# Modulation units moved from the first FFN steps into the first MLP, chunk-by-chunk block starts, and down products two steps behind

## The chip, the cores and the metric

The kernel runs on one core of a Trainium2 chip. The metric is the time of one launch on the device in microseconds, as the median of several runs. The profile shows one further execution of the same program.

## The reference, cut to what matters

`x` has 256 tokens of 1,024 features, all in float32. A first block stack runs over it, then a second one with modulation from a condition vector:

```python
def swiglu(h, w13, w2):
    gate, up = jnp.split(h @ w13, 2, axis=-1)
    return (jax.nn.silu(gate) * up) @ w2
...
x = x + 0.5 * swiglu(rms_norm(x, ffn1_norm[l]), ffn1_w13[l], ffn1_w2[l])   # four FFNs in all, hidden 2816
...
mod = (sc @ w_mod[l] + b_mod[l])[:, None, :]            # sc = silu(c), w_mod[l] is 1024 x 6144, l = 0, 1
sh1, sc1, g1, sh2, sc2, g2 = jnp.split(mod, N_MOD, axis=-1)
...
mod_c = scc @ w_mod[l] + b_mod[l]                       # the context's own modulation, l = 0, first two parts
...
h = h + g1 * y
h = h + g2 * sq_relu_mlp(modulate(rms_norm_2(h, norm2_g[l]), sh2, sc2), w_mlp1[l], w_mlp2[l])  # hidden 4096
```

Between the FFNs stand a recurrent block and a stick-breaking attention; in the second stack, a Fourier and neighbourhood-attention mixer (`l = 0`) and a pooling mixer (`l = 1`), each followed by an MLP.

## The kernel before, in words

**Products.** Features lie on the 128 partitions, in 8 chunks, and tokens on the free axis. Every float32 product is made of three reduced-precision matmuls: high part of the weight by high and by low part of the operand, then low part of the weight by high part (`product`, lines 1471 to 1480). The parts come by splitting: ScalarE writes the rounded high part (`w_hi`, L421), VectorE subtracts it for the low part (`w_lo`, L828).

**The stream.** All weights stand in one stream of 576 units of 128 x 1024 values, in the order of use. SyncE loads them in pairs of 1 MB into a ring of 8 units (`raw`, L348); `w_hi` and `w_lo` are rings of 8 too. A unit's `w_hi` is written only once TensorE has begun the next product unit after the one that had the slot (`unit_used`, `split_hi`). `unit_ready` makes TensorE wait for `w_lo`. Both engines work through the units in order: `pump_to(n)` splits all units up to n, and is written out by hand between the other work of the engine.

**An FFN.** It has 22 steps (`FFS`). Step j has two up units (gate and up columns, 24 matmuls each, `up`), then one down unit (24 matmuls, `down`). Of the up result VectorE makes `t2` with the norm's `rstd` (L965), ScalarE the silu (L479), VectorE the product (L968), ScalarE its high part (L481) and VectorE the low part `hid_lo` (L970): together the hidden tile of step j (`hidden`). The order on TensorE is up j, down j-1: the down product is one step behind. The up results go to PSUM banks 4 and 5 in turn, hidden tiles to two slots, the down sums to banks 0 to 3. `FF_ORDER` lays the units out.

**Block start.** `update_and_operand` (VectorE) and `gain_operand` (ScalarE) add the last block's result to `x` and make the operand of the next one chunk by chunk (`u_hi` L451, `u_lo` L928; L915 in `ffn0` and `ffn2`, L941 in the MLPs), while GpSimd adds up ScalarE's squares (L377, L379). `up(0)` takes its first unit chunk by chunk as the operands arrive, then `norm_sum` sums the squares over the features (one matmul, L1469, bank 7), then come the second unit and `up(1)`. VectorE and ScalarE make `rstd` of the sum (`rms`: L893, the root L443, then L884 to L887), for which `pump_to` has gone up to unit 3 of the FFN. `q`, the first projection of the attention, uses `by_chunk`: of each operand chunk the products of four units are made before the next chunk is taken.

**Modulation.** The two 1024 x 6144 matrices make 96 units of the stream, four to a group of 512 columns, 24 groups. TensorE does not see them: VectorE multiplies the unit's two halves by the condition and adds them to an accumulator, one multiply-add of 128 x 512 to each half (L836 the first, L837 the others, `modulate`); for the context's modulation each half is taken once more (4 groups of `l = 0`). At the end of a group TensorE sums the accumulator over the partitions (`sum_modulation`, four small matmuls, L1547), and VectorE adds the bias (`read_modulation`, L1003). Each FFN has 24 of these units, from step 2 on, in steps 2 to 9 two and one in turn, then one a step (`MODS_AT`); the sums come after the down products of steps 4, 6, 8, 12, 16 and 20. The context's groups are the third and the fourth of `ffn0` and `ffn1`.

**An MLP.** 16 steps (`MLS`) of two up and two down units, matmuls of 258 columns: the two extra ones carry the shift. Up j, down j-1; the up results lie in banks 4 to 7, two each in turn. `sqrelu` starts like an FFN, with `norm_sum` behind the first unit. VectorE reads the shift column (L1036), scales (L1037), ScalarE does the relu (L521), VectorE the square (L1040), then high part (L524) and low part (L1042). There are no modulation units in it.

## Time and profile before

| | us |
|---|---|
| median of 3 runs (1698.51 to 1702.51) | 1699.18 |
| the profiled execution | 1701.26 |
| its span, first to last instruction | 1699.4 |
| TensorE busy (95%) | 1609.3 |
| VectorE busy (71%) | 1200.9 |
| ScalarE busy (46%) | 784.7 |
| GpSimd busy (3%) | 47.0 |

The stretch from the first to the last instruction is the span; the time of a run has some 2 us around it. An engine's busy time is the time in which an instruction of it runs. Matmuls overlap, so the mean duration of one is longer than the distance from one to the next. The granted clock is 1.00 where TensorE runs at 2.4 GHz and 0.50 where it runs at 1.2 GHz; its mean over the span is 0.972.

### The profile page before, as it was taken

To read this page: it belongs to the slowest core of one execution; us is meant where nothing else is said; L and a number is where in the kernel's file an instruction comes from. 1 tells how busy PE (TensorE), PEld (TensorE's weight loads), DVE (VectorE), ACT (ScalarE), POOL (GpSimd) and SP (SyncE) were. 2 spreads that over 40 slices of the span, in tenths; PEclk is the share of its full clock that TensorE was granted. 3 is DMA by queue.
4 is the path that set the end of the run, shared out by engine and by line. 5 is a ranking of instruction groups with operands and counts; after the bars stand their busy time and mean duration, and the time that the engine had idled before them with its cause. 6 is when DMAs were issued, how large, how long until landed. Compare 5 with 4: busy or idle time off the path is not lost.

```text
span 1699.4 us, 30213 instructions
## 1 busy us (share of the span) xinstructions
PE 1609.3 (95%) x12406; PEld 1532.0 (90%) x12406; DVE 1200.9 (71%) x1660; ACT 784.7 (46%) x1121; POOL 47.0 (3%) x46
## 2 busy tenths in 40 slices
PE   6999996899999899999899999998799999889999
PEld 6999996899999799999679999995368999889999
DVE  6887788888878577787767777744757565576654
ACT  5434457543445343445654344422445444454442
POOL 1000010100001100001010000000001000010000
PEclk9999998899999899999999999998899999999999
DMA  6766643466666356565225656531224445334550
GB/s 262 265 245 242 227 169 128 149 250 246 243 231 225 143 198 263 224 233 197 98 100 198 261 223 238 210 124 44 68 87 176 183 173 191 106 122 176 179 191 25
DMA packets 43433, 310.82 MB, mean 183 GB/s; under 512 B 4816, under 2 KB 5072, under 8 KB 6096
## 3 DMA queue, kind: packets, MB, share of 16 engines
q1 hardware_dynamic: 41904, 303.33, 48.0%
q0 software_dynamic: 864, 5.21, 0.9%
q8 instruction: 61, 1.00, 0.2%
q10 hardware_dynamic: 576, 1.05, 0.2%
q14 instruction: 28, 0.23, 0.0%
HBM read 308.52 MB, written 1.05 MB: 182 GB/s over the span
## 4 chain that ended last, share of the span: by engine, by line
PE 67%; DVE 11%; ACT 2%; issue 1%; POOL 0%; POOLq 0%; DVEq 0%; ACTq 0%
PE psum L1474 20%; PE psum L1479 20%; PE psum L1480 20%; DVE w_lo L828 3%; DVE buf L837 1%; ACT w_hi L421 1%; PE psum L1926 1%; PE psum L1649 1%; PE psum L1637 1%; PE psum L1547 1%; DVE u_lo L928 1%; DVE x L907 1%; PE psum L1748 0%; DVE tiny L1380 0%; PE psum L1462 0%
## 5 line engine op out<-in xcount | busy, mean ns | idle before, releaser
L1474 PE MATMUL psum<-u_hi,w_hi 128*128 128x256 f32 (+2 forms) x2608 | 762.4, 292 | 39.1 <-DVE u_lo L915 14.2
L1479 PE MATMUL psum<-u_lo,w_hi 128*128 128x256 f32 (+2 forms) x2608 | 749.8, 287 | 0.0
L1480 PE MATMUL psum<-u_hi,w_lo 128*128 128x256 f32 (+2 forms) x2608 | 749.5, 287 | 0.0
L828 DVE TENSOR_TENSOR w_lo<-raw,w_hi 128x1024 fp32r<-128x1024 f32 x480 | 565.4, 1223 | 163.1 <-ACT w_hi L421 162.9
L1474 PEld LDWEIGHTS psum<-u_hi,w_hi 128*128 128x128 f32 x2608 | 508.1, 195 | 51.0 <-issue 17.3
L421 ACT ACTIVATE w_hi<-raw 128x1024 fp32r<-128x1024 f32 x480 | 478.2, 1046 | 119.6 <-PE psum L1474 112.7
L1479 PEld LDWEIGHTS psum<-u_lo,w_hi 128*128 128x128 f32 x2608 | 508.3, 195 | 2.0
L1480 PEld LDWEIGHTS psum<-u_hi,w_lo 128*128 128x128 f32 x2608 | 507.7, 195 | 1.3
L1474 PE MATMUL psum<-hid_hi,w_hi 128*128 128x256 f32 x1220 | 346.7, 284 | 7.0 <-DVE hid_lo L1357 3.7
L1479 PE MATMUL psum<-hid_lo,w_hi 128*128 128x256 f32 x1220 | 345.6, 283 | 0.0
L1480 PE MATMUL psum<-hid_hi,w_lo 128*128 128x256 f32 x1220 | 345.6, 283 | 0.0
L1474 PEld LDWEIGHTS psum<-hid_hi,w_hi 128*128 128x128 f32 x1220 | 234.4, 192 | 9.8 <-DVE hid_lo L1357 5.5
L1479 PEld LDWEIGHTS psum<-hid_lo,w_hi 128*128 128x128 f32 x1220 | 234.4, 192 | 0.0
L1480 PEld LDWEIGHTS psum<-hid_hi,w_lo 128*128 128x128 f32 x1220 | 234.4, 192 | 0.0
L479 ACT ACTIVATE buf<-buf 128x256 f32<-128x256 f32 x88 | 36.8, 418 | 367.5 <-DVE buf L965 367.5
L837 DVE SCALAR_TENSOR_TENSOR buf<-raw,tiny,buf 128x512 f32<-128x512 f32 x196 | 143.4, 749 | 4.1
L965 DVE TENSOR_TENSOR buf<-psum,rstd 128x512 f32<-128x512 f32 x88 | 60.5, 687 | 30.6 <-PE psum L1480 30.4
L970 DVE TENSOR_TENSOR hid_lo<-buf,hid_hi 128x256 fp32r<-128x256 f32 x88 | 37.5, 426 | 42.7 <-ACT hid_hi L481 42.7
L968 DVE TENSOR_TENSOR buf<-buf 128x256 f32<-128x256 f32 x88 | 37.4, 426 | 42.6 <-ACT buf L479 42.6
L377 POOL TENSOR_TENSOR buf<-buf 128x512 f32<-128x512 f32 x27 | 35.6, 1317 | 1143.4 <-ACT buf L439 1141.0
L521 ACT ACTIVATE buf<-buf,tiny 128x256 f32<-128x256 f32 x64 | 29.1, 502 | 72.8 <-DVE buf L1037 72.8
L481 ACT ACTIVATE hid_hi<-buf 128x256 fp32r<-128x256 f32 x88 | 36.8, 419 | 43.3 <-DVE buf L968 43.3
(224 smaller groups left out, 982.2 us busy)
## 6 DMA issues: line engine op xcount, KB each, us to landing
raw<-stream SPq DMA_DIRECT2D x288, 1024.0 KB, 4.8
buf<-tab POOLq DMA_DIRECT2D x2, 768.0 KB, 4.6
x<-x_in SPq DMA_DIRECT2D x1, 1024.0 KB, 7.0
buf<-ctx_in POOLq DMA_DIRECT2D x1, 1024.0 KB, 5.1
buf<-poolmat POOLq DMA_DIRECT2D x1, 1024.0 KB, 5.0
out<-x ACTq DMA_DIRECT2D x4, 256.0 KB, 2.4
cst<-consts POOLq DMA_DIRECT2D x1, 864.0 KB, 9.1
buf<-late POOLq DMA_DIRECT2D x1, 640.0 KB, 4.5
```

The source lines that it names most:

```text
L377: gp.tensor_tensor(a, a, buf[4][:, half(b)], ALU.add).then_inc(S.pool_sum, 1)
L421: sc.activation(w_hi[:, u], raw[:, u], ACT.Copy).then_inc(S.hi_ready, 1)
L479: sc.activation(sil, t2[:, 0:T], ACT.Silu).then_inc(S.gated, 1)
L481: sc.activation(hid_hi[:, j % 2, 0:T], h32[:, 0:T], ACT.Copy).then_inc(S.hid_hi_ready, 1)
L828: ve.tensor_tensor(w_lo[:, u], raw[:, u], w_hi[:, u].bitcast(F32), ALU.subtract).then_inc(S.lo_ready, 1)
L837: return ve.scalar_tensor_tensor(acc, w, c, acc, ALU.mult, ALU.add)
L965: ve.tensor_tensor(t2.rearrange("p (k t) -> p k t", k=2), bank2(4 + par), over2(rstd[:, :]), ALU.mult).then_inc(S.up_scaled, 1)
L968: ve.tensor_tensor(h32[:, 0:T], sil, t2[:, T:2 * T], ALU.mult).then_inc(S.hid_f32, 1)
L970: ve.tensor_tensor(hid_lo[:, par, 0:T], h32[:, 0:T], hid_hif[:, par, 0:T], ALU.subtract)\
L1474: ins = te.matmul(dst, w_hi[:, w], hi, start=first, stop=False, skip_group_check=True)
L1479: te.matmul(dst, w_hi[:, w], lo, start=False, stop=False, skip_group_check=True)
L1480: return te.matmul(dst, w_lo[:, w], hi, start=False, stop=last, skip_group_check=True)
```

## The change

The groups of modulation units are listed by hand (`GROUPS`) and given to the blocks by `HOME`: 4, 4, 5 and 5 groups to the FFNs, 6 to `mlp0`. In the FFNs they begin at step 6 (in `ffn2` and `ffn3` with two a step in steps 6 to 9, else one), in `mlp0` two a step in steps 3 to 14. The context's groups are the first two of `ffn0` and `ffn1`. In `mlp0` the sums go to column 300 of a bank of the up product just read, and `up_pair` waits for the read of it.

In the FFNs down j-2 comes after up j (`LAG`), the hidden tiles have four slots, and the third up pair has bank 7. `ffn1` to `ffn3` take their first four units chunk by chunk, `ffn0` its first two, the MLPs their first three. `norm_sum` comes after the block, in `ffn0` after `up(1)`, and in these blocks into bank 0. ScalarE and VectorE split the units up to number 7 of an FFN before the root. The scale `G2` is made after `ffn3` instead of after `ffn1`, `H2` after `mlp0`.

```diff
-FFU = 4 * FFS + 2
-MODG = 6
-MODS_AT = [0, 0] + [2, 1] * 4 + [1] * (FFS - 10)
...
+LAG = 2
+GROUPS = [(0, 0), (0, 1), (0, 4), (0, 5), (0, 2), (0, 3), (0, 6), (0, 7), (0, 8), (0, 9), (0, 10), (0, 11)]
+GROUPS += [(1, _n) for _n in range(12)]
+HOME = {"ffn0": range(0, 4), "ffn1": range(4, 8), "ffn2": range(8, 13), "ffn3": range(13, 18), "mlp0": range(18, 24),
+        "mlp1": range(24, 24)}
+CTX_GROUPS = [[0, 1], [4, 5]]
+MODS_AT = {"ffn0": [0] * 6 + [1] * 16, "ffn1": [0] * 6 + [1] * 16, "ffn2": [0] * 6 + [2] * 4 + [1] * 12,
+           "ffn3": [0] * 6 + [2] * 4 + [1] * 12, "mlp0": [0] * 3 + [2] * 12 + [0], "mlp1": [0] * MLS}
+SUM_AT = {"ffn0": [8, 12, 16, 20], "ffn1": [8, 12, 16, 20], "ffn2": [6, 8, 12, 16, 20], "ffn3": [6, 8, 12, 16, 20],
+          "mlp0": [3, 5, 7, 9, 11, 13], "mlp1": []}
+ORDER = {}
+for _name, _mods in MODS_AT.items():
+    assert sum(_mods) == 4 * len(HOME[_name])
+    _lag, _wide = (LAG, 1) if _name[:3] == "ffn" else (1, 2)
+    ORDER[_name] = []
+    for _j, _m in enumerate(_mods):
+        ORDER[_name] += [("up", _j)] * 2 + [("mod", _j)] * _m + [("down", _j - _lag)] * (_wide * (_j >= _lag))
+    for _j in range(len(_mods) - _lag, len(_mods)):
+        ORDER[_name] += [("down", _j)] * _wide
...
-MOD_COLS = [[4, 5, 0, 1, 6, 7], [8, 9, 2, 3, 10, 11], [0, 1, 2, 3, 4, 5], [6, 7, 8, 9, 10, 11]]
...
+def unit_at(name, kind, j):
+    return AT[name] + ORDER[name].index((kind, j))
...
+def end_of(name):
+    return AT[name] + len(ORDER[name])
...
+MOD_ACC, MOD_FREE = {}, {}
+for _name, _groups in HOME.items():
+    for _i, _g in enumerate(_groups):
+        MOD_ACC[_g] = _i % 2 if _name == "mlp0" else int(_i >= len(_groups) - 3)
+        MOD_FREE[_g] = max([g + 1 for g in range(_g) if MOD_ACC[g] == MOD_ACC[_g]], default=0)
 MOD_BACK = {}
...
@@ -113,7 +131,7 @@
 RD = {n: i for i, n in enumerate("ffn0 rec gate wout ffn1 k v ffn2 wo ffn3 k2 fq2 v2 woe mlp0 pool mlp1".split())}
 NORMS = "start ffn0 wout ffn1 ctx ffn2 wo ffn3 woe mlp0 pool".split()
 NRM = {n: i for i, n in enumerate(NORMS)}
-NORM_BANK = {"ffn3": 0}
+NORM_BANK = {n: 0 for n in ("start", "wout", "ctx", "wo", "ffn3", "woe", "pool")}
...
+UP_BANK = [4, 5, 7] + [4 + _j % 2 for _j in range(3, FFS)]
+MOD_COL = 300
...
         hid_hif = hid_hi_t[:, :].bitcast(F32).rearrange("p (s t) -> p s t", s=2)
+        ff_hi = hid_hi_t[:, :].rearrange("p (s t) -> p s t", s=4)
+        ff_lo = hid_lo_t[:, :].rearrange("p (s t) -> p s t", s=4)
...
-                    sc.activation(hid_hi[:, j % 2, 0:T], h32[:, 0:T], ACT.Copy).then_inc(S.hid_hi_ready, 1)
-                pump_to(c0 + ff_at("down", 0) - 1)
+                    sc.activation(ff_hi[:, j % 4, :], h32[:, 0:T], ACT.Copy).then_inc(S.hid_hi_ready, 1)
                 for j in range(FFS - 2):
                     hidden(j)
-                    pump_to(c0 + ff_at("down", j + 1) - 1)
...
                 for j in range(MLS):
                     hidden(j)
-                    pump_to(min(c0 + 4 * j + 5 + AHEAD, last - 1))
+                    pump_to(min(unit_at(name, "up", j + 1) + 1 + RING, last - 1) if j + 1 < MLS else last - 1)
...
@@ -551,7 +574,7 @@
                 square(0, x_t, b)
                 if b == 1:
                     pump_to(3)
-            pump_to(ff_at("down", 0) - 1)
+            pump_to(7)
...
             pump_to(AT["ffn1"] + AHEAD - 1)
-            gain_operand("ffn2_0", "wout", early=AT["ffn1"] + 4)
+            gain_operand("ffn2_0", "wout", early=AT["ffn1"] + 8)
...
@@ -778,6 +801,7 @@
             norm_only("mlp0")
+            act.wait_ge(S.mod_read, HOME["mlp0"][-1] + 1)
             shift_operand(1)
             v = ck(buf[3])
...
-                    ve.tensor_tensor(hid_lo[:, par, 0:T], h32[:, 0:T], hid_hif[:, par, 0:T], ALU.subtract)\
+                    ve.tensor_tensor(ff_lo[:, j % 4, :], h32[:, 0:T], ff_hif[:, j % 4, :], ALU.subtract)\
                       .then_inc(S.hid_ready, 1)
-                pump_to(c0 + ff_at("down", 0) - 1)
                 for j in range(FFS - 2):
                     hidden(j)
-                    pump_to(c0 + ff_at("down", j + 1) - 1)
-                    if j in MOD_READ:
-                        read_modulation(MODG * int(name[3]) + MOD_READ.index(j))
+                    pump_to(unit_at(name, "down", j) - 1)
+                    if j in SUM_AT[name]:
+                        read_modulation(HOME[name][SUM_AT[name].index(j)])
                     if name == "ffn2" and CTX_FROM <= j <= CTX_FROM + NC:
                         context_operand(j - CTX_FROM)
                 hidden(FFS - 2)
-                read_modulation(MODG * int(name[3]) + MODG - 1)
-                pump_to(c0 + FFU + 3)
+                pump_to(end_of(name) - 1)
+                read_modulation(HOME[name][-1])
+                pump_to(end_of(name) + 3)
                 hidden(FFS - 1)
...
@@ -1043,7 +1061,10 @@
                 for j in range(MLS):
                     hidden(j)
-                    pump_to(min(c0 + 4 * j + 5 + AHEAD, last - 1))
+                    pump_to(min(unit_at(name, "up", j + 1) + 1 + RING, last - 1) if j + 1 < MLS else last - 1)
+                    if j in SUM_AT[name]:
+                        read_modulation(HOME[name][SUM_AT[name].index(j)], 4 + 2 * (j % 2), MOD_COL)
...
+            pump_to(7)
...
-            pump_to(AT["ffn1"] + 3)
+            pump_to(AT["ffn1"] + 7)
...
@@ -1416,6 +1439,8 @@
             sqrelu("mlp0")
+            modulation_done("mlp0")
+            scale_gain("H2", 1, 4, "n2_1")
             update_x("mlp0", lambda k: part(0, 5, k))
...
@@ -1466,7 +1491,12 @@
                 pe.wait_ge(S.ssq_ready, POOL_SUMS[name] + 1)
                 if n == 0:
                     pe.wait_ge(S.consts_in, 16)
-                te.matmul(psum[:, 7, 0:T], ones, buf[4][:, 0:T], start=True, stop=True).then_inc(S.ms_psum, 1)
+                if name == "ctx":
+                    pe.wait_ge(S.v_out, 1)
+                te.matmul(psum[:, NORM_BANK.get(name, 7), 0:T], ones, buf[4][:, 0:T], start=True, stop=True)\
+                  .then_inc(S.ms_psum, 1)
...
-            def by_chunk(c, op, dsts, done):
+            def by_chunk(c, op, dsts, done, w=T, shared=True):
                 unit_ready(c + len(dsts) - 1)
@@ -1498,8 +1526,9 @@
                     operand(op, k)
                     for s in range(len(dsts)):
-                        ins = product(dsts[s], c + s, k * P, u_hi[:, k, 0:T], u_lo[:, k, 0:T],
-                                      k == 0 and s % 2 == 0, k == NC - 1, begins=k == (NC - 1 if s else 0))
+                        ins = product(dsts[s], c + s, k * P, u_hi[:, k, 0:w], u_lo[:, k, 0:w],
+                                      k == 0 and (s % 2 == 0 or not shared), k == NC - 1,
+                                      begins=k == (NC - 1 if s else 0))
                         if k == NC - 1 and s % 2:
                             ins.then_inc(done, 1)
                 begun[0] = c + len(dsts) - 1
...
-            def up(c, i, j, par, h0, op=None, between=lambda: None):
-                if not isinstance(j, int) or j >= 2:
+            def up(c, i, j, bank, h0):
+                if not isinstance(j, int) or j > 2:
                     pe.wait_ge(S.up_scaled, h0 + j - 1)
-                all_k(c, i, bank2(4 + par)[:, 0, :], op)
-                between()
-                all_k(c + 1, i, bank2(4 + par)[:, 1, :]).then_inc(S.up_ready, 1)
+                all_k(c, i, bank2(bank)[:, 0, :])
+                all_k(c + 1, i, bank2(bank)[:, 1, :]).then_inc(S.up_ready, 1)
...
             def swiglu(name, norm):
-                c0, h0, g0 = AT[name], STEPS[name], MODG * int(name[3])
-                def down(j, par, c, i=0, first=False, last=False):
+                c0, h0, groups = AT[name], STEPS[name], HOME[name]
+                def down(j, slot, c, i=0, first=False, last=False):
                     pe.wait_ge(S.hid_ready, h0 + j + 1)
-                    one_k(c, i, hid_hi[:, par, 0:T], hid_lo[:, par, 0:T], 0, first, last)
-                up(c0 + ff_at("up", 0), 0, 0, 0, h0, name, between=lambda: norm_sum(norm))
-                up(c0 + ff_at("up", 1), 0, 1, 1, h0)
-                pe.wait_ge(S.ms_ready, NRM[norm] + 1)
-                down(0, 0, c0 + ff_at("down", 0), first=True)
+                    one_k(c, i, ff_hi[:, slot, :], ff_lo[:, slot, :], 0, first, last)
+                first = [bank2(UP_BANK[j])[:, n, :] for j in range(2) for n in range(2)]
+                if name == "ffn0":
+                    by_chunk(c0, name, first[:2], S.up_ready)
+                    up(c0 + 2, 0, 1, UP_BANK[1], h0)
+                else:
+                    by_chunk(c0, name, first, S.up_ready)
+                norm_sum(norm)
                 for j in range(2, 10):
-                    up(c0 + ff_at("up", j), 0, j, j % 2, h0)
-                    down(j - 1, (j - 1) % 2, c0 + ff_at("down", j - 1))
-                    if j in (4, 6, 8):
-                        sum_modulation(g0 + j // 2 - 2, j // 2 - 2, last_unit(g0 + j // 2 - 2))
+                    up(unit_at(name, "up", j), 0, j, UP_BANK[j], h0)
+                    if j == 2:
+                        pe.wait_ge(S.ms_ready, NRM[norm] + 1)
+                    down(j - 2, (j - 2) % 4, unit_at(name, "down", j - 2), first=j == 2)
+                    if j in SUM_AT[name]:
+                        g = groups[SUM_AT[name].index(j)]
+                        sum_modulation(g, 0, last_unit(g))
                 with pe.Fori(0, (FFS - 10) // 4) as i:
                     for s in range(4):
-                        j, c = 10 + 4 * i + s, c0 + ff_at("up", 10 + s)
-                        up(c, 2 * i, j, s % 2, h0)
-                        down(j - 1, 1 - s % 2, c + 3, 2 * i)
+                        j, c = 10 + 4 * i + s, unit_at(name, "up", 10 + s)
+                        up(c, 2 * i, j, 4 + s % 2, h0)
+                        down(j - 2, s, c + 3, 2 * i)
                         if s == 2:
-                            sum_modulation(g0 + 3 + i, 3, c0 + ff_at("mod", 13), 2 * i)
-                if g0 < 2 * MODG:
-                    sum_context(g0 // MODG)
-                down(FFS - 1, 1, c0 + FFU - 1, last=True)
+                            sum_modulation(groups[-3] + i, 1, unit_at(name, "mod", 13), 2 * i)
+                down(FFS - 2, (FFS - 2) % 4, end_of(name) - 2)
+                if name in ("ffn0", "ffn1"):
+                    sum_context(int(name[3]))
+                down(FFS - 1, (FFS - 1) % 4, end_of(name) - 1, last=True)
...
             def sqrelu(name, norm):
                 c0, h0 = AT[name], STEPS[name]
-                def up_pair(c, i, j, par, op=None, between=lambda: None):
-                    if not isinstance(j, int) or j >= 2:
-                        pe.wait_ge(S.up_scaled, h0 + j - 1)
-                    all_k(c, i, psum[:, 4 + 2 * par, 0:TS], op, TS)
-                    between()
-                    all_k(c + 1, i, psum[:, 5 + 2 * par, 0:TS], w=TS).then_inc(S.up_ready, 1)
-                def down(j, par, c, i=0, first=False, last=False):
+                def up_pair(j):
+                    c, par = unit_at(name, "up", j), j % 2
+                    pe.wait_ge(S.up_scaled, h0 + j - 1)
+                    if j - 2 in SUM_AT[name]:
+                        pe.wait_ge(S.mod_read, HOME[name][SUM_AT[name].index(j - 2)] + 1)
+                    all_k(c, 0, psum[:, 4 + 2 * par, 0:TS], w=TS)
+                    all_k(c + 1, 0, psum[:, 5 + 2 * par, 0:TS], w=TS).then_inc(S.up_ready, 1)
+                def down(j, first=False, last=False):
+                    c, par = unit_at(name, "down", j), j % 2
                     pe.wait_ge(S.hid_ready, h0 + j + 1)
                     for n in range(2):
-                        one_k(c + n, i, hid_hi[:, par, n * T:(n + 1) * T], hid_lo[:, par, n * T:(n + 1) * T], 0,
+                        one_k(c + n, 0, hid_hi[:, par, n * T:(n + 1) * T], hid_lo[:, par, n * T:(n + 1) * T], 0,
                               first and n == 0, last and n == 1)
                 pe.wait_ge(S.shift_lo, 1 if name == "mlp0" else 2)
-                up_pair(c0, 0, 0, 0, name, between=lambda: norm_sum(norm))
+                by_chunk(c0, name, [psum[:, 4 + n, 0:TS] for n in range(3)], S.up_ready, TS, False)
+                norm_sum(norm)
+                all_k(c0 + 3, 0, psum[:, 7, 0:TS], w=TS).then_inc(S.up_ready, 1)
                 pe.wait_ge(S.ms_ready, NRM[norm] + 1)
-                up_pair(c0 + 2, 0, 1, 1)
-                down(0, 0, c0 + 4, first=True)
-                with pe.Fori(0, (MLS - 2) // 2) as i:
-                    for s in range(2):
-                        j, c = 2 + 2 * i + s, c0 + 6 + 4 * s
-                        up_pair(c, i, j, s)
-                        down(j - 1, 1 - s, c + 2, i)
-                down(MLS - 1, 1, c0 + 4 * MLS - 2, last=True)
+                down(0, first=True)
+                for j in range(2, MLS):
+                    up_pair(j)
+                    down(j - 1)
+                    if j in SUM_AT[name]:
+                        g = HOME[name][SUM_AT[name].index(j)]
+                        pe.wait_ge(S.up_scaled, h0 + j + 1)
+                        sum_modulation(g, MOD_ACC[g], last_unit(g), bank=4 + 2 * (j % 2), at=MOD_COL)
+                down(MLS - 1, last=True)
```

## Rows read from the trace of the kernel before

**Rows 1.** The page: TensorE's busy time, and one group of the costliest instructions.

```profile
PE 1609.3 (95%) x12406; PEld 1532.0 (90%) x12406; DVE 1200.9 (71%) x1660; ACT 784.7 (46%) x1121; POOL 47.0 (3%) x46
...
L837 DVE SCALAR_TENSOR_TENSOR buf<-raw,tiny,buf 128x512 f32<-128x512 f32 x196 | 143.4, 749 | 4.1
```

**Rows 2.** Windows; stretch: length, busy PE, PEld, DVE, ACT, POOL; PEclk, DMA share, GB/s.

```profile
10.24:30.88 20.64, 16.68 (x99) 15.47 (x100) 15.48 (x19) 12.43 (x19) 5.49 (x5) 1.00 0.62 256
322.39:340.79 18.40, 15.88 (x99) 14.64 (x99) 14.29 (x20) 8.98 (x16) 4.62 (x4) 0.81 0.21 80
587.12:606.14 19.02, 14.58 (x101) 14.20 (x100) 11.81 (x21) 7.06 (x13) 4.51 (x4) 0.82 0.08 31
886.81:903.91 17.10, 14.99 (x92) 13.96 (x93) 12.94 (x17) 7.63 (x13) 4.62 (x4) 0.80 0.00 0
1282.09:1299.51 17.42, 15.03 (x93) 14.08 (x93) 14.71 (x20) 10.20 (x16) 5.28 (x5) 0.80 0.32 121
1504.50:1521.88 17.38, 14.40 (x101) 13.72 (x100) 14.05 (x22) 8.37 (x14) 4.53 (x3) 0.90 0.35 122
```

**Rows 3.** Windows: whole steps of `ffn0`, `ffn1`, the end of `ffn2`, one MLP step.

```profile
79.00:99.50 20.50, 17.57 (x145) 17.20 (x144) 17.46 (x25) 7.34 (x10) 0.00 (x0) 1.00 0.64 239
100.55:136.53 35.98, 35.98 (x290) 35.98 (x289) 30.02 (x42) 14.72 (x20) 0.00 (x0) 0.95 0.68 235
136.53:171.96 35.43, 35.43 (x298) 35.43 (x297) 26.37 (x35) 15.76 (x22) 0.00 (x0) 1.00 0.67 254
388.69:406.61 17.92, 17.37 (x145) 17.17 (x145) 16.32 (x23) 5.26 (x7) 0.00 (x0) 1.00 0.63 226
407.66:442.59 34.93, 34.65 (x288) 34.45 (x289) 29.44 (x41) 14.32 (x19) 0.00 (x0) 1.00 0.67 236
443.64:478.13 34.49, 34.49 (x290) 34.49 (x289) 26.29 (x35) 15.78 (x22) 0.00 (x0) 1.00 0.71 262
784.34:787.98 3.64, 2.88 (x26) 2.68 (x24) 2.61 (x5) 0.83 (x2) 0.00 (x0) 1.00 1.03 407
1360.00:1371.56 11.56, 11.56 (x98) 11.56 (x98) 6.86 (x11) 5.56 (x7) 0.00 (x0) 1.00 0.50 181
```

**Rows 4.** Timeline of TensorE, starts of `ffn0`, `ffn1`: start, duration, instruction [idle <- releaser].

```profile
19.98 0.58 PE L1474 MATMUL psum<-u_hi,w_hi 128*128 128x256 f32 x1
...
322.39 0.36 PE L1474 MATMUL psum<-u_hi,w_hi 128*128 128x256 f32 x1 [1.47 <-DVE u_lo L928]
...
328.50 0.58 PE L1474 MATMUL psum<-u_hi,w_hi 128*128 128x256 f32 x1 [0.41 <-DVE u_lo L928]
...
330.18 1.05 PE L1469 MATMUL psum<-buf,cst 128*128 128x256 f32 x2
```

**Rows 5.** Timeline of VectorE: first hidden tile of `ffn1`, and a step with context.

```profile
335.34 0.69 DVE L965 TENSOR_TENSOR buf<-psum,rstd 128x512 f32<-128x512 f32 x1
...
337.43 0.42 DVE L970 TENSOR_TENSOR hid_lo<-buf,hid_hi 128x256 fp32r<-128x256 f32 x1 [0.48 <-ACT hid_hi L481]
...
424.19 0.69 DVE L965 TENSOR_TENSOR buf<-psum,rstd 128x512 f32<-128x512 f32 x1
...
433.29 0.68 DVE L965 TENSOR_TENSOR buf<-psum,rstd 128x512 f32<-128x512 f32 x1
```

**Rows 6.** Windows at the lower clock: in `ffn1`'s start and before the pooling mixer.

```profile
326.80:333.60 6.80, 6.11 (x24) 5.48 (x25) 4.36 (x5) 2.81 (x3) 2.06 (x2) 0.50 0.01 4
...
1480.50:1487.30 6.80, 4.33 (x14) 3.56 (x15) 4.18 (x11) 3.58 (x8) 0.00 (x0) 0.50 0.00 0
```

**Rows 7.** Timeline: TensorE before the pooling mixer; `mlp1`'s norm sum and first `hid_lo`.

```profile
1482.97 0.69 PE L1953 MATMUL psum<-cst,buf 128*128 128x128 f32 x2 [5.67 <-ACT buf L787]
...
1511.09 1.14 PE L1469 MATMUL psum<-buf,cst 128*128 128x256 f32 x2 [2.19 <-POOL buf L379]
...
1519.47 0.69 DVE L1042 TENSOR_TENSOR hid_lo<-buf,hid_hi 128x512 fp32r<-128x512 f32 x1 [0.70 <-ACT hid_hi L524]
```

**Rows 8.** Timeline of VectorE in `mlp0`: the last split of a step.

```profile
1381.90 1.23 DVE L828 TENSOR_TENSOR w_lo<-raw,w_hi 128x1024 fp32r<-128x1024 f32 x1 [1.68 <-ACT w_hi L421]
```

125 lines of the change are left out of this document (54 added, 71 removed).

## The prediction

> **What bounds the kernel now.** I read the engines' shares first: TensorE is busy for 95% of the span [rows 1]. The weight splitting and the modulation on VectorE run beside it and cost time only where TensorE waits for them. So the question is where TensorE is idle or slow and how much of that the change removes. The stretches of the six block starts, each from the first up matmul to the first down matmul, come next [rows 2]: to read are the stretch, TensorE's busy time and the granted clock. In `ffn1` 18.40 us pass, 15.88 busy, at a mean clock of 0.81, for 96 up matmuls and one sum. At full rate these are worth some 12: a steady stretch of four FFN steps, 288 matmuls without a modulation sum, takes 34.49 us [rows 3], so 0.1198 us a matmul, 2.87 us a unit of 24, 5.75 us an up pair, 8.62 us a step. With one sum the same stretch takes 35.43 us, so a sum costs 0.94. The MLP's step of 96 matmuls takes 11.56 us, 2.89 a unit [rows 3].
>
> At a start the first unit waits chunk by chunk for operands ([1.47 <- DVE] before the first [rows 4]); then the norm's sum of squares is taken; `rstd` and the first hidden tile must follow before the first down product. From the sum's start at 330.18 [rows 4] to the end of `hid_lo` at 337.85 [rows 5] are 7.67 us. The clock stood at its lower level of 1.2 GHz (granted 0.50) from 326.8 to 333.6 [rows 6]. In `ffn2` and `mlp1` TensorE also waits for GpSimd's sum: `mlp1` shows 2.19 [rows 7], and in `ffn2` busy time falls short of the stretch by 4.44 [rows 2].
>
> **FFN starts (`ffn1`, `ffn2`, `ffn3`).** The change takes four units chunk by chunk: 96 matmuls, 11.50 us, 12 matmuls (1.44 us) to an operand chunk, where one unit alone spent 0.36. Operands for the seventh chunk were there at 328.50, 6.1 us after those of the first [rows 4], 1.0 us a chunk and so faster than 1.44: I expect no gap after the first. Then the norm's sum, then `up(2)` (5.75), then the first down product. The chain from sum to `hid_lo` I take at 7.2: the 7.67 less about half of the sum matmul's 1.05, which ran at the lower clock [rows 4]; ends 7.0 and 7.7. TensorE has sum and `up(2)` to do meanwhile, about 6.3, and idles 0.9. The first down product thus comes 11.50 + 7.2 = 18.7 us after the first up matmul; before it came after 18.40, 19.02 and 17.10 [rows 2]. But one more up pair is done by then, 5.75 us of work. Gain: 5.75 - 0.3 = 5.45, 5.75 + 0.3 = 6.05, 5.75 - 1.6 = 4.15, together 15.7.
>
> What is late next: the second down unit. The chunk block keeps its four ring slots to the end, and ScalarE and VectorE split unit 8 only after the second hidden tile. With H the first `hid_lo`: a hidden tile takes 2.51 (335.34 to 337.85 [rows 5]), unit 8 another 1.05 + 1.23 less 0.4 of overlap, the third tile 2.5, unit 9 again 1.9 to 2.3: ready at about H + 9.4. TensorE wants it after one down and one up pair, H + 8.6. I charge 0.8 three times, 2.4 in all; bounds 0 and 2.87 each. Leaves 13.3. The two extra splits ahead of `rms` fall in the chunk block, where VectorE is free, and cost nothing; if GpSimd's sums held them up, up to 3 us are spare.
>
> **`ffn0` start.** It runs at the lower clock from the beginning; the last operand chunk starts at 19.98 [rows 4]. Only two units go by chunk. Six matmuls at about 0.21 follow it, then `up(1)` 5.75 with some 0.5 for the clock: the sum at 27.7, `hid_lo` at 34.9. Before, the first down product stood at 30.88 with 5.75 us less done: gain 1.7, less the same 0.8, makes 0.9; bounds -1 and 3.
>
> **Modulation out of the first six steps.** A step with one unit that also feeds the context takes VectorE 9.10 us (424.19 to 433.29 [rows 5]) against TensorE's 8.62, or 8.86 with a quarter of a sum. Today the units of `ffn0` and `ffn1` start at step 2, two in every other step, and VectorE comes late at the sum of step 8. Two steps took 20.50 instead of 17.24, and the next four 35.98 instead of 34.49 at a clock of 0.95; in `ffn1` 17.92 instead of 17.24 and 34.93 instead of 34.49 [rows 3]. That is 3.26 + 1.49 + 0.68 + 0.44 = 5.9 us. After the change VectorE enters step 6 with nothing owed and runs eight such steps 0.24 behind each, 1.9 us. A sum needs its last unit 11.3 us after the up pair two steps before (down, up pair, down), and VectorE's hidden tile, three splits and one unit need 9.2: the spare 2.1 just covers it. So all 5.9 are gained; bounds 3 and 5.9.
>
> **Two steps behind at the end.** The last hidden tile today leaves TensorE idle 3.64 - 2.88 = 0.76 in `ffn2` [rows 3], and alike in `ffn3`. With two down units (5.75) in between, against the split that now waits for the last up pair (2.3) and the tile (2.5), that is gone: 1.5.
>
> **MLP starts.** Three units go by chunk, 72 matmuls, 8.7 us, and only then comes the sum. Its chain to `hid_lo`, 1511.09 to 1520.16 [rows 7], is 9.07; half a microsecond less at full clock, 8.6. TensorE has only the sum and one unit, 3.5 us, and idles 5.1. The first down product comes after 17.3 us; before after 17.42 and 17.38 [rows 2]. The idle time is thus moved and not removed. And the clock: around 5.67 us idle before 1482.97 [rows 7] it stood at 0.50 from 1480.5 to 1487.3 [rows 6], 4.3 us of that behind the idle time, half of it lost: 2.2. I charge 2.2 for each MLP, 4.4; bounds 0 and 3.4 each.
>
> The Trainium skill, "TensorE: Matmul & The Clock Gate", section "Why this matters for your kernels", warns of idle gaps between bursts of matmuls as what sets the clock back. By it the new gaps in the MLPs are the harm of this change. The trace agrees in the 5.67 us gap; in `ffn1` it shows a fall with no such gap, and what the page would make of that stands with the second rival.
>
> **Modulation in `mlp0`.** Twelve steps get two units each, four multiply-adds of 0.75 us [rows 1], 3.0 us. VectorE is busy 6.86 of 11.56 now [rows 3]; the rest is waiting, 1.68 of it before one split for a ring slot [rows 8], and about 1.9 for ScalarE. With the units it needs 6.9 + 1.9 + 3.0 and 0.1 for the read, 11.9; TensorE with half a sum needs 12.03. I cost this at nothing: it is hidden by the down product that comes a whole step later (7.7 us spare). The sums only move, 24 in all; so do the DMAs of the stream, six units in 12 us against five in 8.9 us in `ffn2`. `H2`'s scale before the update after `mlp0` lies where VectorE waits for the last product: nothing.
>
> **Sum.** 13.3 + 0.9 + 5.9 + 1.5 - 4.4 = 17.2. The profiled execution took 1701.26 us (span 1699.4), so 1684.1. It was 2.1 above the median of the runs, 1699.18, and by that the median would be 1682.0; for small losses that I can't see in the rows I add 1: **1683**.
>
> **Rivals.**
> - *The MLPs keep their clock.* The 2.19 us gap in `mlp1` [rows 7] went with only half as long a fall as the FFNs (mean clock 0.90 against 0.80 [rows 2]). Against it stands the 5.67 row. 4.4 us less: 1679.
> - *The FFN starts fall to the lower clock all the same.* For it: at 326.8 it fell though the one gap of any length was 1.47, before the first matmul, and that stays [rows 4, 6], so a gap alone may not be the cause. Three times 6.8 us at half rate cost 3.4 each, less what the wait for `hid_lo` hides: 1683 + 10 = 1693. By the page's rule on idle gaps, named above, that fall had no gap to come from, and this rival is what it would make of the time.
> - *VectorE still comes late in the context steps.* If the 2.1 us of spare are not there, the sums of step 8 and 12 stall in both FFNs, or the second down unit waits a whole 2.87: some 7 us, 1690.
> - *Slower: `mlp0` goes at VectorE's pace.* If the 4.70 us in which VectorE idles per step today [rows 3] are fixed waits for ring slots and ScalarE, and do not fill with modulation, its step is 14.56 against 12.03; twelve steps lose 30, less 7.7 of look-ahead, 22: 1705. It decides the sign from a VectorE step of about 14.1 on. Against it: those slot waits end at a fixed point of TensorE's progress, so work put in after them delays the next wait and doesn't add to it.
>
> **Numbers.** The forecast gets 0.58, the clock kept 0.12, the clock lost 0.12, VectorE late 0.12, slower 0.06. A measurement of this kernel tells 0.3% from no change, 5.1 us: faster is below 1694.1. All of the first, second and fourth, and half of the third, lie there: 0.88; no change 0.06, slower 0.06. The range runs from the kept clock with the better bounds, 1677, to the lost clock, 1693.
>
> **What would show it.** Right: in `ffn1` to `ffn3` no idle TensorE between the first up matmul and the norm's sum, the first down product 18.7 us after it, full clock; no stall at a sum in `ffn0`; about 5 us idle in both MLP starts, with granted clock 0.50 behind. Wrong: a fall at the FFN starts; waits of TensorE for `w_lo` at the second down unit beyond 1 us; in `mlp0` steps longer than 12.1 us with TensorE waiting for `hid_lo` or a multiply-add.

## The result, and the profile after

| | before | after |
|---|---|---|
| median of the runs | 1698.85 us (1697.87 to 1702.51, 4 runs) | 1675.49 us (1675.29 to 1677.33, 4 runs) |
| profiled execution | 1701.26, span 1699.4 | 1675.29, span 1673.5 |
| mean granted clock | 0.972 | 0.978 |

The ratio is 0.9855, with a 95% interval of 0.9839 to 0.9871. The change gains 23.4 us by the medians and 25.9 by the spans. The forecast was 16.2 and 1683; 1675.5 lies 1.5 below its range.

The page of the changed kernel, busy time of the engines and the group that answers to the second of [rows 1]:

```profile
PE 1591.8 (95%) x12406; PEld 1520.4 (91%) x12406; DVE 1202.9 (72%) x1660; ACT 783.8 (47%) x1121; POOL 49.1 (3%) x46
...
L861 DVE SCALAR_TENSOR_TENSOR buf<-raw,tiny,buf 128x512 f32<-128x512 f32 x196 | 143.5, 749 | 5.3 <-DVE buf L861 0.5
```

TensorE executes the same 12406 matmuls, and VectorE's work has not changed (1202.9 against 1200.9). So the whole gain is idle time and clock. The clock's part can be estimated from the mean granted clock: 1699.4 x (1 - 0.972) = 47.6 us before, 1673.5 x (1 - 0.978) = 36.8 after. That is some 10.8 of the 25.9. TensorE's idle time by the pages fell by 8.4 (1699.4 - 1609.3 = 90.1 before, 1673.5 - 1591.8 = 81.7 after). The other 6.7 or so must lie in what counts as busy, since matmuls overlap: pauses shorter than the modelled end of one, and the beginning of `ffn0`, for which the clock row is of no use.

The granted clock is on record only from its first change on, and the windows over this beginning say 1.00 in both kernels, while the matmuls themselves come 0.21 us apart up to 22.9 before and up to 13.4 after, and 0.12 apart behind. TensorE's timeline there, two lines of the kernel before, then two of the changed one:

```profile
22.71 0.41 PE L1480 MATMUL psum<-u_hi,w_lo 128*128 128x256 f32 x1
23.08 0.28 PE L1479 MATMUL psum<-u_lo,w_hi 128*128 128x256 f32 x1
...
13.11 0.41 PE L1509 MATMUL psum<-u_lo,w_hi 128*128 128x256 f32 x1
13.62 0.28 PE L1509 MATMUL psum<-u_lo,w_hi 128*128 128x256 f32 x1
```

Windows of the changed kernel over the starts of the four FFNs and of `mlp0`, first up matmul to first down matmul (their edges are up to 0.1 us off those matmuls), in the order of [rows 2] and with its columns:

```profile
10.12:33.80 23.68, 20.26 (x146) 19.32 (x146) 18.29 (x22) 13.46 (x21) 5.54 (x5) 1.00 0.80 315
312.86:331.70 18.84, 17.93 (x146) 17.68 (x146) 14.29 (x20) 9.93 (x17) 4.69 (x4) 1.00 0.37 130
567.63:586.55 18.92, 18.01 (x149) 17.76 (x147) 13.66 (x21) 8.08 (x14) 6.29 (x4) 1.00 0.27 102
858.80:877.60 18.80, 17.89 (x148) 17.63 (x146) 14.21 (x20) 9.84 (x17) 4.70 (x4) 1.00 0.21 76
1247.30:1264.61 17.31, 12.26 (x98) 12.00 (x98) 14.88 (x22) 9.98 (x18) 5.34 (x5) 0.95 0.40 147
```

In `ffn1` 146 matmuls are done in 18.84 us, where 98 were done in 18.40, and the granted clock is 1.00 instead of 0.81. That is the core of the change in one pair of rows.

Windows over the rest of the blocks, first down matmul to the first update of x; first two of the kernel before (`ffn0`, `ffn1`), then the same two, `mlp0` and `mlp1` of after:

```profile
30.88:219.60 188.72, 185.79 (x1538) 185.27 (x1537) 148.56 (x198) 77.42 (x105) 0.00 (x0) 0.99 0.67 249
340.79:525.77 184.98, 184.15 (x1538) 183.75 (x1537) 145.72 (x195) 77.43 (x105) 0.00 (x0) 1.00 0.67 249
```

```profile
33.80:209.96 176.16, 176.09 (x1472) 176.12 (x1472) 134.76 (x177) 76.58 (x104) 0.00 (x0) 1.00 0.62 233
331.70:507.86 176.16, 176.09 (x1472) 176.12 (x1473) 134.76 (x177) 76.58 (x104) 0.00 (x0) 1.00 0.61 233
...
1264.61:1444.42 179.81, 179.16 (x1472) 178.99 (x1473) 135.56 (x175) 81.06 (x105) 0.00 (x0) 0.99 0.65 246
1494.80:1667.74 172.94, 172.87 (x1424) 172.90 (x1425) 98.11 (x116) 78.43 (x101) 0.00 (x0) 0.99 0.41 147
```

Behind the first down product no FFN has an idle TensorE any more: 176.09 busy of 176.16 in `ffn0`, where 2.9 us were missing, and as little is missing in `ffn2` and `ffn3`. `mlp0` now executes six sums more, 5.6 us, and the mean clock behind both MLP starts is 0.99.

TensorE's timeline of the changed kernel in `ffn1` and at the first down products of the MLPs (start, duration, instruction [idle <- releaser]):

```profile
312.86 0.36 PE L1504 MATMUL psum<-u_hi,w_hi 128*128 128x256 f32 x1 [1.47 <-DVE u_lo L951]
...
324.45 0.60 PE L1498 MATMUL psum<-buf,cst 128*128 128x256 f32 x2
...
331.77 0.36 PE L1504 MATMUL psum<-hid_hi,w_hi 128*128 128x256 f32 x1 [0.98 <-issue]
...
1264.69 0.55 PE L1504 MATMUL psum<-hid_hi,w_hi 128*128 128x256 f32 x1 [5.13 <-issue]
...
1494.87 0.55 PE L1504 MATMUL psum<-hid_hi,w_hi 128*128 128x256 f32 x1 [5.16 <-issue]
```

Taking the first down product and the first update of x of each block in both traces as marks, with a unit at 2.87, an up pair at 5.75 and a sum at 0.94 us (forecast, from [rows 3]), the span's gain is made up so:

| part | forecast | measured |
|---|---|---|
| starts of `ffn1`, `ffn2`, `ffn3` | 15.7 - 2.4 = 13.3 | 5.2 + 7.4 + 5.2 = 17.9 |
| start of `ffn0` | 0.9 | 2.8 |
| rest of the four FFNs (modulation, two steps behind) | 5.9 + 1.5 = 7.4 | 4.9 + 1.2 + 0.7 + 0.9 = 7.7 |
| both MLPs | -4.4 | -0.4 - 1.5 = -1.9 |
| all other stages | 0 | -0.6 |
| sum | 17.2 | 25.9 |

(The parts are rounded.) For `ffn1`, for example: its first down product came at 340.79 and 331.77, the update of x before it at 320.50 and 310.97. The stretch between grew by 0.51, with one up pair more in it: 5.75 - 0.51 = 5.24.

### The profile page after: what moved, and what is told of

Same layout as the page of the kernel before. It is cut to its first block, busy times and chain, and to the rows that moved or that the text cites. A ratio compares the mean times of both kernels' runs of the same rounds, so it can differ in the third digit from the quotient of the medians.

```text
span 1673.5 us, 30069 instructions
## 1 busy us (share of the span) xinstructions
PE 1591.8 (95%) x12406; PEld 1520.4 (91%) x12406; DVE 1202.9 (72%) x1660; ACT 783.8 (47%) x1121; POOL 49.1 (3%) x46
## 4 chain that ended last, share of the span: by engine, by line
PE 75%; DVE 5%; issue 1%; ACT 1%; DVEq 0%; ACTq 0%
PE psum L1504 23%; PE psum L1509 22%; PE psum L1510 22%; DVE w_lo L852 1%; PE psum L1576 1%; PE psum L1688 1%; PE psum L1676 1%; PE psum L1965 1%; PE psum L1904 1%; ACT w_hi L444 0%; PE psum L1787 0%; DVE tiny L1403 0%; PE psum L1487 0%; PE psum L1945 0%; PE psum L2004 0%
## 5 line engine op out<-in xcount | busy, mean ns | idle before, releaser
L1504 PE MATMUL psum<-u_hi,w_hi 128*128 128x256 f32 (+2 forms) x2608 | 752.1, 288 | 28.9 <-DVE u_lo L938 12.6
L1504 PEld LDWEIGHTS psum<-u_hi,w_hi 128*128 128x128 f32 x2608 | 501.7, 192 | 36.4 <-issue 17.0
L1509 PEld LDWEIGHTS psum<-u_lo,w_hi 128*128 128x128 f32 x2608 | 501.9, 192 | 1.7
L1510 PEld LDWEIGHTS psum<-u_hi,w_lo 128*128 128x128 f32 x2608 | 501.7, 192 | 1.3
L502 ACT ACTIVATE buf<-buf 128x256 f32<-128x256 f32 x88 | 36.8, 418 | 317.4 <-DVE buf L987 317.4
L504 ACT ACTIVATE hid_hi<-buf 128x256 fp32r<-128x256 f32 x88 | 36.8, 418 | 43.3 <-DVE buf L990 43.3
```

The source lines that it names most:

```text
L502: sc.activation(sil, t2[:, 0:T], ACT.Silu).then_inc(S.gated, 1)
L504: sc.activation(ff_hi[:, j % 4, :], h32[:, 0:T], ACT.Copy).then_inc(S.hid_hi_ready, 1)
L1504: ins = te.matmul(dst, w_hi[:, w], hi, start=first, stop=False, skip_group_check=True)
L1509: te.matmul(dst, w_hi[:, w], lo, start=False, stop=False, skip_group_check=True)
L1510: return te.matmul(dst, w_lo[:, w], hi, start=False, stop=last, skip_group_check=True)
```

## The experiments

All are edits of the changed kernel. Their own medians stand beside the ratio to the kernel before on the same chip, since the kernel before itself had medians of 1699 to 1703 us there; the ratio is the safer of the two. The changed kernel's is 0.9855.

### Each of three parts undone alone

**The old places of the modulation units** (all 96 in the FFNs, from step 2 on):

```
-MODS_AT = {"ffn0": [0] * 6 + [1] * 16, ...
+MODS_AT = {f"ffn{_f}": [0, 0] + [2, 1] * 4 + [1] * 12 for _f in range(4)}
+MODS_AT.update({"mlp0": [0] * MLS, "mlp1": [0] * MLS})
```

> The changed kernel with the modulation units back in steps 2 to 21 of the four FFNs, as before the change (groups, context groups and accumulators too). Theory: the new places are worth the 5.9 us that the rows of ffn0 and ffn1 showed, so 1675.5 + 5.9 = 1681.4, with TensorE waiting at the sum of step 8 in ffn0. Rival A: the down product two steps behind takes up VectorE's lateness by itself, and the places are worth nothing: 1675 to 1677. Rival B: units from step 2 on also collide with the late ring slots behind the chunk block, some 2 us more in each FFN: about 1690.

Measured: 1706.65 us, ratio 1.0037 (1.0024 to 1.0050). Undoing 5.9 us of the forecast cost 31. Timeline of this kernel, the split of the first down unit in `ffn1` (VectorE), then the product that waited for it:

```profile
345.88 3.50 DVE L851 TENSOR_TENSOR w_lo<-raw,w_hi 128x1024 fp32r<-128x1024 f32 x3 [0.52 <-ACT w_hi L444]
```

```profile
347.26 0.55 PE L1502 MATMUL psum<-hid_hi,w_hi 128*128 128x256 f32 x1 [5.19 <-DVE w_lo L851]
```

Part of it comes from how the two edits meet. With down products two steps behind, units at step 2 stand ahead of the first down unit; by the code it became the ninth unit instead of the seventh, so that it needs a slot of the ring again, and its split starts only behind the second hidden tile. TensorE idled 5.19 us in each FFN, and the clock fell at the end of it each time. By the marks of the table above, 17.2 of the 30.4 us of span lie in the four starts and 11.6, besides the sums, in the rest of the FFNs. So this run doesn't price the places alone, and the next one was made for that.

**The old number of units, but none ahead of the first down unit:**

```
+MODS_AT = {f"ffn{_f}": [0, 0, 0] + [2, 2, 2, 2, 1, 2, 1] + [1] * 12 for _f in range(4)}
```

> All 96 modulation units are again in the four FFNs, 12 of each 24 in the steps with index 3 to 9, but none ahead of the first down unit, which stays the seventh unit (with the old places it was the ninth, and its low part came 4.2 us late). Theory by the terms of the forecast (modulation in the early steps costs 5.9, its place at the start is what cost the first experiment the rest): 1675.5 and 5.9, about 1681.5, no idle time of 5 us ahead of the first down products and no fall of the clock there. Second reading (the bodies of the FFNs in the first experiment lost 11.5 us beside their sums): 1687. Rival (modulation in these steps puts VectorE behind whatever its place at the start): 1695 or more.

Measured: 1706.07 us, ratio 1.0024 (1.0013 to 1.0035). The time is the rival's. The starts are as in the changed kernel (0.98 us idle), so the loss is in the rest of the blocks. Windows of this kernel over the same stretch of `ffn0` and `ffn1`, and over 26 us inside `ffn1`:

```profile
33.80:220.78 186.98, 181.49 (x1487) 180.89 (x1488) 146.00 (x196) 76.58 (x104) 0.00 (x0) 0.98 0.64 242
342.48:531.00 188.52, 180.57 (x1486) 179.54 (x1487) 146.14 (x196) 76.58 (x104) 0.00 (x0) 0.99 0.63 240
...
377.00:403.00 26.00, 23.32 (x194) 22.98 (x193) 21.39 (x33) 10.70 (x15) 0.00 (x0) 1.00 0.67 241
```

`ffn1` takes 188.52 us against 176.16, of which 7.95 are an idle TensorE, 1.9 the two sums that came back, and the rest mostly clock. Before the change `ffn1` held as many units and idled 0.83 (184.98 with 1538 matmuls, above). Where TensorE waits is on record too. VectorE's timeline of this kernel in `ffn1`, then a product that waited:

```profile
346.66 0.48 DVE L859 TENSOR_SCALAR buf<-raw,tiny 128x512 f32<-128x512 f32 x1
347.17 2.41 DVE L860 SCALAR_TENSOR_TENSOR buf<-raw,tiny,buf 128x512 f32<-128x512 f32 x3
...
353.90 0.35 PE L1502 MATMUL psum<-hid_hi,w_hi 128*128 128x256 f32 x1 [2.36 <-DVE w_lo L851]
```

The 2.36 stand ahead of the second down unit, and there is such a wait in all four FFNs: two modulation units now lie between it and the first, and their four multiply-adds delay its split. That is the place where the forecast charged its 0.8, and where the changed kernel does not wait. The other waits in `ffn1` (0.23 to 2.19 us) stand ahead of later down products and one sum. So both layouts of the old number collide with the late first down units, each in its own way, and this one packs two units a step into steps 3 to 6 besides, where the kernel before had two and one in turn. Neither shows what the old places would cost without such a collision.

**The same, but with the first six steps free and nothing in `mlp0`:**

```
+MODS_AT = {f"ffn{_f}": [0] * 6 + [3] * 4 + [1] * 12 for _f in range(4)}
```

> The first six steps of each FFN hold no modulation, as in the changed kernel, but nothing goes to mlp0: the steps 6 to 9 take three units each, so that all 24 of an FFN are placed. It tells the two halves of the new placement apart. If leaving the early steps is what counts: near the changed kernel, 1677 to 1681. If VectorE's load in the rest of the FFN decides (9.1 us with one unit and context, 3 us more with three, against TensorE's 8.6 to 9.1 a step): four steps owe some 13 us, of which the two-steps-behind order and the spare of the steps before cover 5 to 8, so 5 to 8 us are lost in each of four FFNs: 1697 to 1707, with TensorE waiting for sums or low parts in steps 7 to 12.

Measured: 1718.4 us, ratio 1.0110 (1.0095 to 1.0126): worse than either reading. VectorE's timeline of this kernel in `ffn1`, and the sum that it held up:

```profile
403.57 8.42 DVE L860 SCALAR_TENSOR_TENSOR buf<-raw,tiny,buf 128x512 f32<-128x512 f32 x12
411.91 0.15 DVE L1022 TENSOR_TENSOR mod<-psum,prm 128x4 f32<-128x4 f32 x1
```

```profile
412.21 0.99 PE L1574 MATMUL psum<-cst,buf 128*128 128x2 f32 x4 [6.08 <-DVE mod L1022]
```

Twelve multiply-adds run in a row, 8.42 us, and TensorE waits 6.08 for the read of the sum behind them. So leaving the first six steps is not enough: with the old number the rest of the FFN gets too dense, and a part has to leave the FFNs. What the free first steps are worth by themselves stays open, as no run puts the new, smaller number into them.

**Down products one step behind:**

```
-                    down(j - 2, (j - 2) % 4, unit_at(name, "down", j - 2), first=j == 2)
+                    down(j - 1, (j - 1) % 4, unit_at(name, "down", j - 1))
```

> The changed kernel with the down product one step behind again (chunk block, places of the modulation kept). Theory: the gain at an FFN start is the up pair that TensorE does while rstd is made. Without it the idle time in each start goes from 0.98 to about 6.7 us, 4 x 5.75 = 23 us, with a fall of the clock behind each (about 2 us, as behind the 5.1 us in the MLPs) and 1.5 us at the ends of ffn2 and ffn3: 1675.5 + 23 + 8 + 1.5 = 1708. Rival: the chunk block is what gains, by ending the gaps between operands and the low clock, and the lag adds little: 1680.

Measured: 1708.46 us, ratio 1.0043 (1.0026 to 1.0059). The theory had 1708; that it agrees to the microsecond is partly luck, as it put the clock at a round 2 us an FFN. TensorE's timeline, first down product of `ffn1`:

```profile
340.04 0.55 PE L1504 MATMUL psum<-hid_hi,w_hi 128*128 128x256 f32 x1 [6.72 <-issue]
```

Without an up pair between sum and first down product nothing covers the 7.2 us chain: 6.72 idle, and the clock is low for 6.8 or 10.2 us from within this gap on, in each FFN.

**FFN starts by unit:**

```
-                    by_chunk(c0, name, first, S.up_ready)
-                norm_sum(norm)
+                by_chunk(c0, name, first[:1], S.up_ready)
+                norm_sum(norm)
+                all_k(c0 + 1, 0, first[1]).then_inc(S.up_ready, 1)
+                up(c0 + 2, 0, 1, UP_BANK[1], h0)
```

> The changed kernel with the FFN starts as before: only the first unit chunk by chunk, then the norm's sum, then the other units; down products two steps behind. Theory: the lag alone keeps the 5.75 us a start, but the gaps between operands, the wait for GpSimd's sum and the low clock return: per FFN the 2.5 to 4.4 us of idle time and 3.4 us of clock less the 0.98 that goes, 5 + 7 + 4.5 + 1 = 17 us: 1692. Rival: the idle time was only moved, since the chain to the first hidden tile then begins 7 to 8 us earlier; half of it is hidden: 1683. The old kernel's clock fall should be seen again in ffn1 at granted 0.50.

Measured: 1699.51 us, ratio 0.9993 (0.9983 to 1.0002). 17 were expected, 24 came. Window of this kernel over the start of `ffn1`, then VectorE's first `hid_lo` in it:

```profile
316.20:340.70 24.50, 22.47 (x145) 21.09 (x146) 16.95 (x23) 11.79 (x20) 4.63 (x4) 0.79 0.28 103
```

```profile
331.70 0.42 DVE L992 TENSOR_TENSOR hid_lo<-buf,hid_hi 128x256 fp32r<-128x256 f32 x1 [0.48 <-ACT hid_hi L504]
```

Nothing waits for the hidden tile here: it is ready at 332.1, and TensorE reaches the first down product at 340.86. The same matmuls take 24.50 us instead of 18.84. Of these 5.7 us some 5 are clock, (1 - 0.79) x 24.5. By unit, TensorE has 0.36 us of work to an operand chunk and pauses in between; with four units to a chunk no pause is left behind the first, and the clock stays. In `ffn2` 6.11 us of idle time before the norm's sum come on top (4.44 before).

### The new places alone

Down products one step behind, FFN and MLP starts by unit, and the units split ahead as before.

```
-            pump_to(7)
+            pump_to(3)
```
(beside the edits of the two experiments above and that of the next)

> The new places of the modulation units alone: down products one step behind, FFN and MLP starts by unit as before, units split ahead as before. Theory by the terms of the forecast (the places are worth 5.9 us by themselves): 1698.9 less 5.9, 1693. Rival (the three parts pay only together, as each of them undone alone gave back 24 to 33 of 23): 1698 or more.

Measured: 1694.56 us, ratio 0.9954 (0.9934 to 0.9974), span 1691.1: a gain of about 8 us against the forecast's 5.9, which lies inside the interval (4.4 to 11). This kernel's seven executions range from 1688.9 to 1698.5. Window over the rest of `ffn1`:

```profile
333.43:515.20 181.77, 181.77 (x1521) 181.77 (x1520) 136.09 (x178) 77.41 (x105) 0.00 (x0) 1.00 0.62 231
```

TensorE is never idle in it, and so it is in `ffn0`. So the term was right in kind. With the new places in all four, the spans of block and lag make a square:

| | one step behind | two steps behind |
|---|---|---|
| starts by unit | 1691.1 | 1698.4 |
| starts by chunk block | 1706.5 | 1673.5 |

The block alone costs 15 us, two steps behind alone 7, both together gain 18; by the ratios, which rest on all executions, it is 15, 7 and 17. The cells differ a little beside the two edits (MLP starts and units split ahead are those of before in the first cell); the next run shows what the MLP starts are worth.

### The MLP starts

**By unit, as before:**

```
-                by_chunk(c0, name, [psum[:, 4 + n, 0:TS] for n in range(3)], S.up_ready, TS, False)
+                by_chunk(c0, name, [psum[:, 4, 0:TS]], S.up_ready, TS, False)
```

> The changed kernel with the MLP starts as before: first unit chunk by chunk, then the norm's sum, then three units. Theory: in the MLPs the chunk block only moves the idle time, and the fall of the clock behind it costs more than the one before: mlp0 loses about 1 us by the block and mlp1 about 2, so without it 1672.5. Rival: the chunk block gains in the MLPs too, because the first down product came 1.4 us earlier in mlp0 than the stretch of before says: 1677 or more.

Measured: 1676.23 us, ratio 0.9858 (0.9836 to 0.9880), span 1672.6: no clear difference from the changed kernel. In `mlp0` the first down product comes 1.5 us later relative to the stage before, and the rest is 2.2 shorter, with no fall of the clock in it (there is one in the start instead, from 1253.5 to 1260.3); in `mlp1` the start is as long as with the block and the rest 1.5 shorter. By stage the start by unit is thus 2.2 us better, near the theory's 3; neither the span (0.9 less) nor the medians show it clearly. For the MLPs the chunk block is worth nothing or a little less.

**Fillers that keep TensorE busy in the MLPs' idle time** (42 matmuls in each, whose result is not used):

```
+                for m in range(42):
+                    te.matmul(psum[:, 1, 0:T], w_hi[...], u_hi[...], start=True, stop=True, ...)
                 pe.wait_ge(S.ms_ready, NRM[norm] + 1)
```

> Behind the fourth up unit of each MLP start 42 matmuls of 128x256 into an unused bank are added, 5 us at full clock, so that TensorE is busy in the 5.13 and 5.16 us in which it waits for the root; their result is not used. Theory (the clock falls for 6.8 us in mlp0 and 3.4 us in mlp1 because of that idle time, and half of such a stretch is lost): 3.4 and 1.7 us come back, 1675.5 to 1670.5. Rival (the clock falls for another reason, or the fillers push the down products back by as much): no change, 1675 to 1677.

Measured: 1671.59 us, ratio 0.9830 (0.9812 to 0.9847), span 1669.7, 3.8 less; the intervals of the two ratios still touch, so the windows carry the reading. Windows over the rest of `mlp0` and `mlp1`:

```profile
1263.90:1441.56 177.66, 176.99 (x1473) 176.79 (x1473) 135.45 (x176) 81.13 (x105) 0.00 (x0) 1.00 0.65 249
1492.40:1663.85 171.45, 171.33 (x1423) 171.36 (x1424) 98.01 (x117) 78.35 (x101) 0.00 (x0) 1.00 0.42 148
```

The granted clock is 1.00 in both, and they are 2.15 and 1.5 us shorter (179.81 and 172.94 above). That is what the fall behind the idle time costs: 3.65 us, with 4.4 forecast.

**The norm's sum inside the chunk block** (behind the sixth chunk index):

```
+                    if between and k == at:
+                        between()
...
+                    by_chunk(c0, name, first, S.up_ready, between=lambda: norm_sum(norm), at=5)
```

> The matmul that sums the squares stands inside the chunk block (behind the sixth of eight chunk indices) in place of behind it, in ffn1 to ffn3 and in both MLPs; in ffn0 it stands ahead of the second pair of up units. In the changed kernel TensorE is idle 0.98 us before each FFN's first down product and 5.13 and 5.16 us in the MLP starts, each time at the end of the chain sum, root, hidden tile. Theory (that chain alone ends the starts, and it begins with the sum): the sum comes 1 to 2 us earlier, the four gaps of 0.98 us close and those of the MLPs shrink by about 2 us each: 1675.5 less 3.9 less 4, about 1668. Rival (the chain is set by VectorE's last operand chunks, with which the sum's input is ready only just before the block ends): under 1 us, 1674.5 to 1675.5.

Measured: 1670.26 us, ratio 0.9805 (0.9788 to 0.9821), span 1668.5. Of the 8 us forecast 5 came. Timeline of this kernel, the sum in `ffn1` and the first down product of `mlp1`:

```profile
320.28 0.60 PE L1498 MATMUL psum<-buf,cst 128*128 128x256 f32 x2
...
1491.30 0.36 PE L1504 MATMUL psum<-hid_hi,w_hi 128*128 128x256 f32 x1 [3.15 <-issue]
```

All four gaps of 0.98 in the FFNs are gone, `mlp1`'s 5.16 became 3.15, but `mlp0`'s 5.13 only 4.66. There the sum is done by 1253.0, but VectorE takes its result up at 1254.72, behind two splits:

```profile
1252.45 2.35 DVE L852 TENSOR_TENSOR w_lo<-raw,w_hi 128x1024 fp32r<-128x1024 f32 x2
1254.72 0.41 DVE L916 TENSOR_SCALAR nrm<-psum 128x256 f32<-128x256 f32 x1
```

So the theory (the sum alone sets the chain) holds for the FFNs and `mlp1` and not for `mlp0`, where an earlier sum meets a busy VectorE. In this profile the clock did not fall behind the 3.15.

**Sum inside the block and fillers in `mlp0`, then in both MLPs** (38 and 26 matmuls):

> The sum inside the chunk block (as in the run before it) and 38 filler matmuls behind the fourth up unit of mlp0 only, where 4.66 us of idle time were left with a fall of the clock of 6.8 us behind; in mlp1 3.15 us were left and no fall. Theory (clock and sum pay apart): the block with the sum inside gave 5.0 us of span, the fillers in mlp0 2.2: 1675.5 less 7.2, about 1668.3, and no stretch at the lower clock between 1255 and 1445. Rival (the fall only moves to another place): 1670 to 1671, as without the fillers.

> As the last run with the sum inside the block and fillers, with 26 filler matmuls in the start of mlp1 as well, where 3.15 us of idle time were left and the clock fell for 6.8 us behind it in one profile and not in another. Theory: no stretch at the lower clock behind either MLP start; against the run with fillers in mlp0 alone 2.8 us of mlp1's body come back: span 1669.3 to some 1665, below both kernels compared here. Rival (the fillers delay the down product, or the clock falls elsewhere): 1668 or more.

Measured: 1668.54 us, ratio 0.9815 (0.9799 to 0.9831), and 1669.09 us, ratio 0.9815 (0.9802 to 0.9829). In the first profile `mlp0` kept its clock, but 3.15 us of idle time in `mlp1` now had a fall of 6.8 us behind it, which the run before did not have. In the second both kept it, and the profiled execution took 1663.8 (span 1662.0, clock 0.984); the other four took 1667.6 to 1669.2 at 0.978 or 0.979. So on top of the sum inside the block the fillers show nothing in the medians. All three variants are 5 to 7 us below the changed kernel by the medians and 7 to 9 by the ratios; which of them is best these runs don't tell.

### VectorE's room in `mlp0`

**Three units a step in eight steps instead of two in twelve:**

```
-  "mlp0": [0] * 3 + [2] * 12 + [0],
+  "mlp0": [0] * 3 + [3] * 8 + [0] * 5,
```

> The 24 modulation units of mlp0 stand three to a step in the steps 3 to 10, in place of two in twelve steps. It tests at which load VectorE sets the step. By the terms of the forecast (its waits of 1.9 us a step for ScalarE and slots do not fill): 6.9, 1.9, 4.5 and 0.1 make 13.4 a step against 12.0 to 12.2 for TensorE, eight steps lose 10 and the look-ahead covers 7.7: some 2 to 3 us, 1678. If the waits fill with modulation work, VectorE needs 11.5 and nothing is lost: 1675.5. If even two units a step were near the limit (the slower rival of the forecast, 4.7 us of fixed waits): 16.2 a step, 33 less 8, 1700.

Measured: 1677.55 us, ratio 0.9874 (0.9859 to 0.9889), span 1674.4. Window of this kernel inside `mlp0`:

```profile
1290.00:1365.00 75.00, 75.00 (x628) 75.00 (x627) 63.89 (x88) 32.84 (x42) 0.00 (x0) 1.00 0.75 282
```

TensorE has no idle time at three units a step, and in all of `mlp0` it waits only where the changed kernel waits too (5.14 ahead of the first down product, 0.56 ahead of the last). The slower rival is refuted by a wide margin. Of VectorE's waits a part filled with work and a part did not. Its groups in the same window:

```profile
L852 DVE TENSOR_TENSOR w_lo<-raw,w_hi 128x1024 fp32r<-128x1024 f32 x25 | 29.0, 1218 | 1.1 <-ACT w_hi L444 1.1
L1060 DVE TENSOR_TENSOR hid_lo<-buf,hid_hi 128x512 fp32r<-128x512 f32 x6 | 4.2, 692 | 4.2 <-ACT hid_hi L546 4.2
L1058 DVE TENSOR_TENSOR buf<-buf 128x512 f32<-128x512 f32 x6 | 4.2, 692 | 5.9 <-ACT buf L543 5.9
```

The waits ahead of splits are nearly gone (1.1 us in 75). The two waits for ScalarE inside a hidden tile stay, 10.1 us for six tiles, 1.7 a step. So the reading was about right that 1.9 us a step do not fill. But VectorE's work came to some 10.5 a step (63.89 in the 6.1 steps of this window), not 11.5, and with the waits it just keeps TensorE's pace.

## Why the prediction was right and wrong

**FFN starts, right in kind.** The forecast had the first down product 18.7 us after the first up matmul, a chain of 7.2 from sum to `hid_lo`, 0.9 idle and full clock. Measured, from matmul to matmul: 18.91 in all three; 324.45 to 331.67, so 7.2; 0.98; 1.00. Gross 15.7 was forecast; the stretches give 5.24, 5.86 and 5.23. Two things in it were off.
- *The start of `ffn3` was placed wrongly.* [Rows 2] has 886.81:903.91, apparently taken from the first up matmul that shows a wait. Two operand chunks earlier, at 885.52, stands the first one. Before the change the stretch took 18.4, not 17.10, and the term was 1.1 too small. The same slip in `mlp0` (from 1280.61 on, 18.9 instead of 17.42) hid a gain of 1.5.
- *The clock ahead of `ffn2`.* Of `ffn2`'s 7.4, 1.6 lie ahead of its first up matmul: a low-clock stretch in the products before it was 6.8 us long at 569.1 and is 3.4 long at 552.7. Nothing in the forecast spoke of it. Whether the change caused it is open: among kernels that don't differ up to there it is 3.4 us long in one profile (the MLP starts by unit) and absent in another (the fillers).

**The second down unit, wrong.** This is the step that failed. The forecast charged 0.8 us four times (2.4 and 0.8) for a wait for unit 9's low part. No such wait exists in any of the four FFNs. VectorE's timeline of the changed kernel:

```profile
331.24 0.43 DVE L992 TENSOR_TENSOR hid_lo<-buf,hid_hi 128x256 fp32r<-128x256 f32 x1 [0.48 <-ACT hid_hi L504]
...
338.79 2.36 DVE L852 TENSOR_TENSOR w_lo<-raw,w_hi 128x1024 fp32r<-128x1024 f32 x2 [0.52 <-ACT w_hi L444]
```

With the first `hid_lo` at H = 331.67, the unit is split at 338.79 + 1.18, H + 8.3; the step had said H + 9.4. TensorE wants it at 331.77 + 8.62, H + 8.7, so it is 0.4 early. Its splits took 1.7 us each behind the tile (337.84 + 0.42 to 339.97), where the step had 1.9 and 1.9 to 2.3; and its own terms add up to 8.8 to 9.2, not to 9.4. This was the largest single error, 3.2 us, and it hung on a difference of a few tenths between two sums of 8 to 9 us: such a charge is a bound and no term.

**`ffn0`.** The sum was put at 27.7 and `hid_lo` at 34.9. They came at 26.56 and 33.77: the two-unit block was done by 20.8, not at 21.5, and the up pair behind it ran at full clock, without the 0.5 set aside. The premise that failed is the clock: the forecast kept it low up to the sum, as it was before the change (up to 22.9), and with two units to a chunk it rose at 13.4. That is 1.1 us more gain. With the charge of 0.8 that makes 2.8 instead of 0.9, within the bounds given.

**Modulation out of the first six steps, right.** 5.9 and the 1.5 of the two-steps-behind ends were forecast, 7.7 measured, and `ffn0` and `ffn1` gave 4.9 and 1.2 where 4.75 and 1.1 were forecast; the places alone gave 8 with a wide interval. What the forecast missed is that the parts depend on each other. It priced them as a sum. But with the old number of units in the FFNs, block and two steps behind give 1706, not 1681: the places are worth 8 us in the kernel before and 30 in the changed one, as laid out in the two experiments, in which modulation units collide with the first or the second down unit. This did not spoil the number, because all parts are made together; it would have spoiled every forecast of one part.

**Two steps behind at the end, right.** 0.76 us of idle time in `ffn2` and `ffn3` are gone.

**MLPs.** 5.1 us of idle time in each and a lower clock behind it, as forecast: 5.13 and 5.16. The fall costs 2.15 and 1.5 us, against 2.2 twice. The rest of the difference is the misplaced start of `mlp0` named above. Net -1.9 instead of -4.4.

**The rivals.** *The MLPs keep their clock*: fell. *The FFN starts fall to the lower clock*: fell, 1.00 in all four. The Trainium skill, "TensorE: Matmul & The Clock Gate", section "Why this matters for your kernels", blames idle gaps between bursts; the experiments agree more than the forecast did, with a fall behind each of the gaps of 4.7 to 6.7 us shown above and none where fillers took them away. But the start by unit falls as well, with pauses of only 0.36 to 1.46 us in `ffn1`; on that the rule of this section is silent. *VectorE late in context steps*: fell for the new places; no sum waited. *Slower, `mlp0` at VectorE's pace*: fell; with three units a step TensorE still does not wait.

**The sum.** 8.7 us were missing: 3.2 for the second down unit, 2.6 for the two misplaced starts, 1.6 for the clock ahead of `ffn2`, 1.1 in `ffn0`, 0.8 for the clock in the MLPs, 0.3 in the rest of the FFNs, less 0.6 in other stages; that is 9.0, of which the stretches' 5.24 and 5.86 against 5.45 and 6.05 take back 0.4, and rounding the rest. The extra 1 us "for small losses" went the wrong way. Nearly all errors were on the cautious side, and together they reached past the range. The charges stayed within their bounds. The misplaced starts and the clock ahead of `ffn2` had no bounds, and that the latter fell in the change's favour may be chance; without its 1.6 the time would have lain just inside the range.

## What to carry to other kernels

When parts of a change work on one bottleneck from several sides, price the corners of the square and not its edges: here the chunk block without the second lag costs 15 us, the lag without the block 7, and both gain 18. VectorE is busy 71 and 72% of the two kernels, and yet TensorE waited nearly 8 us for it in one FFN once modulation units stood in other places. The share says nothing about that; look at what stands in such an engine's queue ahead of the piece that the bottleneck needs next. And count a start's short pauses as clock too: of the gain in span some two fifths were granted clock.

## What was unexpected of the hardware

- The clock fell at a start by unit with pauses of only 0.36 to 1.46 us (granted mean 0.79 over 24.5 us), and stayed at 1.00 over the same matmuls with one such pause ahead of them. No run here varied the pauses alone. Nor are pauses all there is: ahead of `ffn2`, where some matmuls are on 16 partitions, it fell in the kernel before with TensorE busy throughout, as far as busy time doesn't hide short pauses (windows, clock third from the end):

```profile
561.00:569.00 8.00, 8.00 (x58) 7.58 (x58) 4.27 (x7) 6.10 (x7) 0.00 (x0) 1.00 0.01 3
569.00:576.00 7.00, 7.00 (x27) 5.96 (x26) 5.57 (x7) 1.06 (x1) 0.00 (x0) 0.51 0.12 39
```

- Whether it falls behind 3.15 us of idle time is not fixed: in one profile of the kernel with the sum inside the block it did not, in the next kernel with the same gap it fell for 6.8 us. The executions of the kernel with fillers in both MLPs range over 5 us (1663.8 to 1669.2), and go with the mean clock, 0.984 to 0.978.
